# Two programs of a hybrid network reordered: stacked filter products in the first, norm and projection of two layers merged and computed with halves

## The reference, cut to what matters

```python
# first block: modulation, projection, filters of the long convolutions
mod_l = (jax.nn.silu(c) @ w_mod[i] + b_mod[i])[:, None, :]
p_l = modulate(rmsnorm(h_lat, norm1[i]), sh1_l, sc1_l) @ w_in[i]
...
h = jnp.sin(sin_freq[1] * (h @ w2 + b2))
h = (h @ w3).astype(f32).reshape(seqlen, HY_ORDER, 2, HY_WIDTH)
h = h * jnp.exp(-t * deltas)[:, None, None, :]
...
k = jnp.concatenate([h_fwd, jnp.zeros_like(h_fwd[:1]), h_bwd[:0:-1]], axis=0)
k_f = jnp.fft.rfft(k, axis=0)
```

## Time and profile before

| | |
|---|---|
| Median of 3 runs | 3527.74 us (3522.45 to 3529.1) |
| Profiled execution, its time | 3524.44 us |
| Profiled execution, its span (first to last instruction) | 3522.5 us |
| Mean granted TensorE clock | 0.935 of full speed |
| Busy: PE, DVE, ACT | 3140.0, 2403.8, 1708.7 us |

### The profile page before, as it was taken

The page is one execution under the profiler, slowest core; times in us unless marked ns, Lnnn a source line. Parts: engine busy times, 40 slices in busy tenths (PEclk is TensorE's granted clock), DMA queues, the critical chain, the costliest instruction groups (busy, mean ns, idle before and its releaser), DMA issues. The chain is left out here.

```text
span 3522.5 us, 49529 instructions
## 1 busy us (share of the span) xinstructions
PE 3140.0 (89%) x16784; PEld 2578.4 (73%) x16785; DVE 2403.8 (68%) x3602; ACT 1708.7 (49%) x2103; POOL 41.5 (1%) x47
## 2 busy tenths in 40 slices
PE   6899886888989999967969976868999999999998
PEld 2578543887968899965848964837888888888886
DVE  3555751589968666644735524737899989989997
ACT  2434310344733443423314413306888888887886
POOL 0000000000000000000000000000000000000000
PEclk9999798899999999988989987988999999999999
DMA  6453022443577666632016421019999999999995
GB/s 227 162 206 108 1 90 107 152 144 132 207 246 242 215 209 208 209 123 74 1 48 228 165 103 44 1 63 382 348 381 371 357 352 379 376 352 384 363 363 185
DMA packets 225418, 731.87 MB, mean 208 GB/s; under 512 B 23479, under 2 KB 59753, under 8 KB 222825
## 3 DMA queue, kind: packets, MB, share of 16 engines
q1 hardware_dynamic: 221352, 702.32, 54.8%
q0 software_dynamic: 2768, 23.59, 2.3%
q10 hardware_dynamic: 1152, 4.19, 0.3%
HBM read 702.24 MB, written 28.84 MB: 208 GB/s over the span
## 5 line engine op out<-in xcount | busy, mean ns | idle before, releaser
L3008 DVE TENSOR_TENSOR moe_lo<-moe_raw,moe_hi 128x1024 fp32r<-128x1024 f32 x756 | 886.0, 1221 | 55.7 <-ACT moe_hi L2861 36.4
L2861 ACT ACTIVATE moe_hi<-moe_raw 128x1024 fp32r<-128x1024 f32 x756 | 787.7, 1060 | 148.4 <-PE moe_pB L2811 79.3
L2811 PE MATMUL moe_pB<-moe_hi,moe_hEh 128*128 128x512 f32 x1008 | 399.8, 397 | 3.9 <-DVE moe_hEl L3004 3.9
L2811 PE MATMUL moe_pB<-moe_hi,moe_hEl 128*128 128x512 f32 x1008 | 394.2, 391 | 0.0
L2811 PE MATMUL moe_pB<-moe_lo,moe_hEh 128*128 128x512 f32 x1008 | 393.5, 390 | 0.0
L1412 PE MATMUL route_pS<-fh,route_uh 128*128 128x256 f32 x640 | 190.7, 298 | 36.0 <-DVE route_ul L1515 35.8
L2811 PEld LDWEIGHTS moe_pB<-moe_hi,moe_hEh 128*128 128x128 f32 x1008 | 190.0, 188 | 41.7 <-issue 4.1
L2811 PEld LDWEIGHTS moe_pB<-moe_hi,moe_hEl 128*128 128x128 f32 x1008 | 189.8, 188 | 40.7
L2811 PEld LDWEIGHTS moe_pB<-moe_lo,moe_hEh 128*128 128x128 f32 x1008 | 190.2, 189 | 38.0
L1747 PE MATMUL exp_pO<-exp_vh,exp_ah 128*128 128x512 f32 x512 | 201.1, 393 | 4.8 <-DVE exp_al L1806 4.7
L1747 PE MATMUL exp_pO<-exp_vl,exp_ah 128*128 128x512 f32 x512 | 200.6, 392 | 0.0
(11 more groups left out here) (708 smaller groups left out, 6577.2 us busy)
## 6 DMA issues: line engine op xcount, KB each, us to landing
moe_raw<-in_moe_w SPq DMA_DIRECT2D x758, 512.0 KB, 6.5
exp_vs<-in_peer_v SPq DMA_DIRECT2D x128, 512.0 KB, 4.6
route_us<-in_peer_u SPq DMA_DIRECT2D x64, 512.0 KB, 3.3
exp_us<-in_peer_u SPq DMA_DIRECT2D x64, 512.0 KB, 5.0
inp_w<-in_w_mod SPq DMA_DIRECT2D x48, 512.0 KB, 6.5
inp_w<-in_w_tiles SPq DMA_DIRECT2D x40, 512.0 KB, 5.8
gates<-route_big POOLq DMA_DIRECT2D x8, 2048.0 KB, 7.5
exp_gs<-gates SPq DMA_DIRECT2D x32, 512.0 KB, 5.8
```

Source lines behind the costliest of these rows:

```text
L2811: i = pe.matmul(pB[:, kind], l[:, kd], m[:, n % HALVES, ns], start=kd == 0 and x == 0, stop=kd == KD - 1 and x == 2)
L2861: act.activation(hi[:, n % HALVES], raw[:, n % RING], ACT.Copy).then_inc(hi_ready, 1)
L3008: dve.tensor_tensor(lo[:, n % HALVES], raw[:, n % RING], hi[:, n % HALVES], ALU.subtract).then_inc(lo_ready, 1)
```

## The change

In the first program the hidden rows for forward and backward filter are stacked: `hid_sum` holds both, `hid_diff` the second with its sign turned (one more pair of sines), and a single 128-row product by the stacked W3 gives sum and difference at once. DVE only multiplies by the decay. The first tap of the backward half is cleared in the hidden rows. The order of filter rows, spectra, modulation and transposes is another on all engines: the last three spectra stand behind the transposes, and the halves of the normalized tokens are made between them. The transposes use two banks. `keep_rows` stands ahead of `silu` and `high`. Gate and column steps come two tiles later. Three loads are issued later.

In the later layers one program `stage_norm_z` replaces norm and projection. The first four weight tiles are loaded from its start, the ring has four slots, both sides are split into halves, all products are products of halves, and the loops are written out.

The diff, cut to its core:

```diff
-        arg, kk, hid = (early[:, n:n + T] for n in (2560, 2816, 3072))
+        arg, kk, hid_sum, hid_diff = (early[:, n:n + T] for n in (2560, 2816, 3072, 3328))
...
-        hf, hb = filt[:, 0], filt[:, 1]
-        hs, hd = (filt[:, 2], filt[:, 3]), (filt[:, 4], filt[:, 5])
+        hs, hd = (filt[:, 0], filt[:, 1]), (filt[:, 2], filt[:, 3])
...
+                    if n == at_block["tile", 2]:
+                        for g, at in ((g1bc, GATE1 * D), (g2bc, GATE2 * D)):
+                            sp.dma_start(g[:], b_mod[0, at:at + D].partition_broadcast(P)).then_inc(bg_loaded, 16)
+                        sp.dma_start(wd[:], w_dt).then_inc(wd_loaded, 16)
...
                     cs = slice(half * BANK, (half + 1) * BANK)
                     if n or a:
                         pe.wait_ge(f_read, 2 * n + a)
-                    for d in range(2):
-                        i = pe.matmul(pp[d][:], hid[d * HID:(d + 1) * HID, a * P:(a + 1) * P], W3[d * HID:(d + 1) * HID, o, cs], start=True, stop=True)
...
 
                 def spectrum(n, ft):
...
-                    if kd:
-                        pe.wait_ge(t_read, kd)
+                    if kd == 1:
+                        pe.wait_ge(f_read, 8)
+                    if kd >= 2:
+                        pe.wait_ge(t_read, kd - 1)
                     for a in range(2 * TT):
                         src = x_tok[:, a] if a < TT else ctok[:, a - TT]
-                        i = pe.transpose(pt[:, a * P:(a + 1) * P], src[:, kd * P:(kd + 1) * P], k.ident[:])
+                        i = pe.transpose(ptx[kd % 2][:, a * P:(a + 1) * P], src[:, kd * P:(kd + 1) * P], k.ident[:])
...
-                pe.matmul(parg, W2, hid[0:HID], start=True, stop=True).then_inc(arg_psum, 1)
-                pe.wait_ge(sin_ready, 2)
-                pe.wait_ge(filt_loaded, 64)
+                pe.matmul(parg, W2, hid_sum[0:HID], start=True, stop=True).then_inc(arg_psum, 1)
+                pe.wait_ge(hid_ready, 1)
+                pe.wait_ge(w3_loaded, 32)
                 filter_rows(0, 0)
                 filter_rows(0, 1)
+                filter_rows(1, 0)
+                pe.wait_ge(dft_loaded, 16)
+                spectrum(0, 0)
+                filter_rows(1, 1)
+                spectrum(0, 1)
                 pe.wait_ge(c_ready, 1)
-                spectrum(0, 0)
-                filter_rows(1, 0)
                 mod_rows(0)
-                spectrum(0, 1)
-                filter_rows(1, 1)
+                filter_rows(2, 0)
                 spectrum(1, 0)
-                filter_rows(2, 0)
+                filter_rows(2, 1)
                 mod_rows(1)
                 spectrum(1, 1)
-                filter_rows(2, 1)
+                filter_rows(3, 0)
+                pe.wait_ge(c_loaded, 16)
+                mod_columns(SHIFT)
                 spectrum(2, 0)
-                filter_rows(3, 0)
                 mod_rows(2)
+                filter_rows(3, 1)
                 pe.wait_ge(xn_ready, 1)
                 transposes(0)
                 transposes(1)
+                mod_rows(3)
+                for kd in range(2, KD):
+                    transposes(kd)
+                mod_columns(SCALE)
                 spectrum(2, 1)
-                filter_rows(3, 1)
-                transposes(2)
-                transposes(3)
-                pe.wait_ge(c_loaded, 16)
-                mod_columns(SHIFT)
                 spectrum(3, 0)
-                transposes(4)
-                transposes(5)
-                mod_rows(3)
                 spectrum(3, 1)
-                transposes(6)
-                transposes(7)
-                mod_columns(SCALE)
-                pe.wait_ge(s_read, 8)
-                pe.wait_ge(f_read, 8)
...
-                    if q in (4, 16):
-                        mod_gate(GATE1 if q == 4 else GATE2)
-                    if q in (8, 12):
-                        if q == 8:
+                    if q in (6, 18):
+                        mod_gate(GATE1 if q == 6 else GATE2)
+                    if q in (10, 14):
+                        if q == 10:
                             pe.wait_ge(gate_ready, 1)
-                        mod_columns(SHIFT2 if q == 8 else SCALE2)
+                        mod_columns(SHIFT2 if q == 10 else SCALE2)
...
                 act.wait_ge(arg_ready, 2)
-                act.activation(hid, arg, ACT.Sin).then_inc(sin_ready, 1)
+                act.activation(hid_sum, arg, ACT.Sin).then_inc(sin_ready, 1)
+                act.activation(hid_diff[0:HID], arg[0:HID], ACT.Sin)
+                act.activation(hid_diff[HID:2 * HID], arg[HID:2 * HID], ACT.Sin, scale=-1.0).then_inc(sin_ready, 1)
```

The rest of the first program, ScalarE and VectorE:

```diff
+                keep_spectrum(0, 0)
+                act.wait_ge(x_loaded, 32)
+                square(0)
+                square(1)
+                keep_spectrum(0, 1)
+                square(2)
+                square(3)
+                keep_spectrum(1, 0)
+                act.wait_ge(mean_ready, 1)
+                act.activation(rt[:], ms[:], ACT.Sqrt).then_inc(root_ready, 1)
+                keep_rows(SHIFT)
+                keep_spectrum(1, 1)
+                keep_spectrum(2, 0)
+                keep_x(0)
+                keep_x(1)
+                keep_rows(SCALE)
+                for kd in range(2, KD):
+                    keep_x(kd)
+                high(0)
+                act.wait_ge(scale_ready, 1)
+                high_h(0)
+                high_h(1)
+                keep_spectrum(2, 1)
+                high(1)
+                high_h(2)
+                high_h(3)
+                keep_spectrum(3, 0)
+                high_h(4)
+                high_h(5)
+                high(2)
+                keep_spectrum(3, 1)
+                high_h(6)
+                high_h(7)
...
+                        if q in (3, 7, 11, 15):
+                            keep_rows(GATE1 + q // 4)
...
-                    if q in (3, 7, 11, 15):
-                        keep_rows(GATE1 + q // 4)
...
+                dve.wait_ge(sin_ready, 2)
+                c.tick(dve.memset(hid_sum[HID:2 * HID, 0:1], 0.0))
+                dve.wait_ge(sin_ready, 3)
+                dve.memset(hid_diff[HID:2 * HID, 0:1], 0.0).then_inc(hid_ready, 1)
+                dve.wait_ge(dec_loaded, 16)
 
                 def filters(n):
                     cs = slice(n % 2 * BANK, (n % 2 + 1) * BANK)
+                    if n >= 2:
+                        dve.wait_ge(s_psum, 2 * n - 2)
                     for a in range(TT):
                         dve.wait_ge(f_psum, 2 * n + a + 1)
-                        c.tick(dve.tensor_tensor(hf[:, a], pp[0][:], dec[:, a, cs], ALU.mult))
-                        c.tick(dve.tensor_tensor(hb[:, a], pp[1][:], dec[:, a, cs], ALU.mult))
-                        c.settle()
-                        dve.nop().then_inc(f_read, 1)
-                    c.link(dve.memset(hb[0:1, 0, :], 0.0))
-                    if n >= 2:
-                        dve.wait_ge(s_psum, 2 * n - 2)
-                    c.tick(dve.tensor_tensor(hs[n % 2], hf, hb, ALU.add))
-                    c.link(dve.tensor_tensor(hd[n % 2], hf, hb, ALU.subtract))
-                    dve.nop().then_inc(filt_ready, 1)
+                        dve.tensor_tensor(hs[n % 2][:, a], pp[0][:], dec[:, a, cs], ALU.mult)
+                        dve.tensor_tensor(hd[n % 2][:, a], pp[1][:], dec[:, a, cs], ALU.mult).then_inc(f_read, 1)
...
-                filters(2)
+                columns_of(SHIFT)
                 filters(3)
-                columns_of(SHIFT)
                 columns_of(SCALE)
```

The merged program of the later layers:

```diff
+                for n in range(RING):
+                    sp.dma_start(w[:, n], w_a[n]).then_inc(w_loaded[n], 16)
+                for n in range(RING, ZT):
+
+                    sp.wait_ge(wl_ready, n - RING + 1)
+                    sp.dma_start(w[:, n % RING], w_a[n]).then_inc(w_loaded[n % RING], 16)
+                    if n == RING + 1:
+                        sp.dma_start(wb[:], w_b).then_inc(b_loaded, 16)
+                    if n == RING + 3:
+                        sp.dma_start(wc[:], w_c).then_inc(c_loaded, 16)
...
+                pe.wait_ge(xn_ready, 1)
+                for n in range(KD // 2):
+                    if n >= 2:
+                        pe.wait_ge(hl_ready, n - 1)
+                    for j in range(4):
+                        kd, a = 2 * n + j // 2, j % 2
+                        i = pe.transpose(pt[:, n % 2, j * P:(j + 1) * P], xn[:, a, kd * P:(kd + 1) * P], k.ident[:])
+                    i.then_inc(t_psum, 1)
+                for n in range(ZT):
+                    pe.wait_ge(wl_ready, n + 1)
+                    if n >= AHEAD:
+                        pe.wait_ge(raw_ready, n - AHEAD + 1)
+                    for kd in range(KD):
+                        if n == 0 and kd % 2 == 0:
+                            pe.wait_ge(hl_ready, kd // 2 + 1)
+                        for j, (a, b) in enumerate(((wh, hh), (wh, hl), (wl, hh))):
```

(81 more changed lines are left out.)

150 lines of the change are left out of this document (51 added, 99 removed).

## The result

The changed kernel takes 3435.37 us (median of four executions, 3430.53 to 3444.07). The kernel before, run beside it, takes 3525.09. The ratio is 0.9755, with a 95% interval of 0.974 to 0.9769. The forecast was 3439, range 3422 to 3459. The median fell by 89.7 us, the forecast said 88.7.

The account below looks back on a forecast made before the run. TensorE was taken as the bound, with waits and half-clock stretches in the prologue, tiles and later layers; gains 26 + 18.8 + 19.3 + 24.6 = 88.7 from 3524.4 give 3435.7, plus 3.3 for the median: 3439, range 3422 to 3459.

Parts of the forecast that it names:

- Prologue, 29.0 before the deduction: First program: the modulation step behind tile 1 starts at 96.4 instead of 125.42, 29.0 us less; 26 was taken.
- Filter rows 1.1: Prologue: each filter row behind the first spectrum takes 1.1 us on TensorE; the first three, at half clock, 2.08 each.
- 5 of them because tile 0 ran at half clock: Prologue: 5 of the 29.0 us gained come from tile 0 having run at half clock before.
- gone from the path: Prologue: VectorE's sum, difference and clearing of the filters (two of 1.225 us and small ones) leave the path for all four n.
- The deduction of 3 for the clock: Prologue: 3 us taken off the 29.0 because transposes ahead of the last three spectra may lower the clock.
- rival A: Prologue loses the clock behind the transposes and gains only 19 us; time 3446; chance 0.14.
- Convolution tiles, 18.8: Seven tile pairs take 96.7 instead of 115.46 us: 10.1 of waits at three stops, the rest half clock behind each.
- Rival C: Convolution tiles: the three stops come back as load waits, costing 12 of the 18.8 us; time 3451; chance 0.08.
- Layer 0, 19.3, and layer 1, 24.6: Merged norm and projection: layer 0 ends at 1615.6 instead of 1634.9, layer 1 takes 65.4 instead of 90.0 us.
- Rival B: Merged program: slower chain of halves, 3.5 us a tile and 3.0 a wide step, 8.4 a layer; time 3456; chance 0.12.
- Rival D: Later layers: weight loads stand in front of each product of halves, 128 us more; time 3567; chance 0.02.
- Anything else in the kernel moving: Listed sign that the forecast is wrong: a change in time in parts of the kernel not edited.

Follow-up runs that it names:

- the two repeats: The changed kernel, unedited, run again twice against the kernel before: 3432.07 us (ratio 0.9738) and 3433.25 us (ratio 0.9751).
- no_stack: Changed kernel with the filter stacking undone (separate products, VectorE clears, adds and subtracts again) in the new prologue order: 3423.23 us, ratio 0.9734.
- stack_old_order: First program of the kernel before with stacking as its only edit, later layers merged as in the changed kernel: 3468.17 us, ratio 0.9859.
- stops_back: Changed kernel with both convolution-tile edits undone (late copy of modulation rows, gate and column steps two tiles earlier): 3453.35 us, ratio 0.9819.
- three_slots: Changed kernel with three slots instead of two for the weight halves in the merged program: 3426.66 us, ratio 0.9738.
- layers_only: Kernel before with only the merged norm and projection of the two later layers, first program old: 3478.67 us, ratio 0.9874.

## Why the prediction was right, point by point

The time came within 4 us, and the mechanisms of the tiles and the layers stood as told. The mechanism of the prologue did not: there errors cancel. That the median fell by 89.7 where I had 88.7 is in part luck, too. The profiled execution fell by 84.3, and in the two repeats the median fell by 94.1 and 88.3.

- *Prologue, 29.0 before the deduction: measured 28.7, with wrong terms in it that cancel.* "Filter rows 1.1" was taken from rows of 64-row products and put on stacked ones of 128 rows, which measured 1.88. That is about 0.7 on each of the five rows behind the first spectrum. Against it, the first spectrum took 3.60 where I had 5.8, and rows and spectra begin a little before the one ahead ends, where I had added their full lengths; so the first transposes came at 61.77 where I had 61.1. Tile 0 started at 84.49 where I had 85.4, and tiles 0 and 1 took 12.3 where I had 11.0. The reading "5 of them because tile 0 ran at half clock" is too high: of tile 0's 10.5 us before, the clock made about 3 (13 products 0.45 apart instead of 0.23), and some of the rest was waiting for the low halves of the tokens (0.40 and 0.41). The claim that with VectorE's sum and difference "gone from the path" the stacking helps is wrong in this order: `no_stack` has them back and is 1.5 us earlier at the modulation step. The new order alone (with the banks and loads that go with it) gives 29.2, the stacking alone 10.9, and both together 27.7: in the new order the stacking costs. I never priced the two separately.
- *The deduction of 3 for the clock: not needed.* The three spectra behind the transposes ran in 3.68, 3.67 and 3.70. The Trainium skill ("TensorE: Matmul & The Clock Gate", Part 4, PE-mode transpose) made the deduction certain; this trace does not agree, with 1.00 in both windows around the six transposes that follow one another (65.76 to 69.86). It was no idle fear, though: `stack_old_order` lost the clock behind transposes and a column step with no wait ahead of the spectrum. What decides between the two cases stays open; rival A, which would have put the step near 106, did not occur in any of the eleven profiles with the new order, whose step came at 95.3 to 98.7.
- *Convolution tiles, 18.8: measured 19.1.* Right in cause, and in size within the 3.1 us that `stops_back` does not bring back: it brings 16.0 back, and each edit alone takes all of it. Rival C (load waits) is refuted: ACT's wait grew to 9.09, and PE did not stop.
- *Layer 0, 19.3, and layer 1, 24.6: measured 20.5 and 25.1* (19.2 and 25.0 by the second profile). The clock at the start makes the difference between the profiles: in the first it rose 1.2 us after tile 0 began, in the second 4.3 us. The wide step was sized at 2.57 and took 2.69, and a third slot brings it to 2.53 (`three_slots`): with two slots the hand-over costs more than the mean of chain and products. Rival B (3.5 a tile, 3.0 a step) is refuted by 2.96 and 2.69. Rival D is refuted by 0.119 a product with its load; the rule of the Trainium skill ("TensorE: Matmul & The Clock Gate", Part 3, What overlaps and what doesn't) would, by the estimate in the prediction (107 ns for each of the layer's 336 products), have made layer 0 longer by 36 us, and the measurement decides against it.
- *"Anything else in the kernel moving"* was named as a sign of error, and it came: the scan by 8.8 in this execution. It goes with a lower granted clock in this execution, the repeats had it at 2.9 and 5.9, and `layers_only`, with nothing edited up to its end, at 3.1. Whether the change has a share in it is open. With the longer scan the profiled execution is the second slowest of its four and 4.8 above the median; against the forecast's sum it lost the 8.8 and gained 2.7 in the prologue, 0.3 in the tiles and 1.7 in the layers.

## What to carry to other kernels

An edit that takes work off an engine and an edit that hides the same work are substitutes: price each alone, then both. Take a matmul's price from a row of the same shape in both operands; two products of 64 rows in different halves of the array cost less than two of 128 rows. And where an untouched program moves by some per cent, profile the same kernel again before looking for a cause.

## What was not expected of the hardware

- Two float32 products of 64 rows and 512 columns, in different row halves, took 1.13 us together; two of 128 rows took 1.88. At the start of the program it was 2.08 and 3.78, while the windows there give a granted clock of 1.00.
- The granted clock of one untouched program differs between executions of one kernel: 0.53 and 0.61 in the same 20 us, and 120.7 and 114.8 us for the program. The kernel before, with 0.91 there, took 111.9.
- A column step and transposes stood ahead of a spectrum in both orders. In the old order with the stacking the spectrum took 5.38 us (clock 0.72), in the new order 3.68 (1.00).
